# Local attention by chunk pairs with head pairs in the rows, instead of masked 128-token blocks

## The reference, cut to what matters

```python
qc = q.reshape(Bsz, n_chunks, CHUNK, B_KV_HEADS, groups, HEAD_DIM)
kb, vb = band(kc), band(vc)            # own chunk and the one before: 128 keys
scores = einsum('bcqhgd,bckhd->bchgqk', qc, kb) * (HEAD_DIM ** -0.5)
scores = where(valid, scores, -inf)    # the first chunk has none before it
m = maximum(max(scores, -1), sink)
p = exp(scores - m)
probs = p / (sum(p, -1) + exp(sink - m))
out = einsum('bchgqk,bckhd->bcqhgd', probs, vb)
```

## Time and profile before

| | |
|---|---|
| median of the runs | 906.06 us |
| the three runs | 903.81, 906.06, 906.17 us |
| span of the profiled execution, first to last instruction | 902.6 us |
| mean granted TensorE clock | 0.964 of full |
| busy: PE, PEld, DVE, ACT, POOL | 835.4, 678.3, 591.8, 410.8, 185.4 us |
| DMA | 144.43 MB, mean 160 GB/s |

### The profile page before, as it was taken

The page is one execution under the profiler, slowest core; times in us unless marked ns, Lnnn a source line. Parts: engine busy times, 40 slices in busy tenths (PEclk is TensorE's granted clock), DMA queues, the critical chain, the costliest instruction groups (busy, mean ns, idle before and its releaser), DMA issues.

```text
span 902.6 us, 11887 instructions
## 1 busy us (share of the span) xinstructions
PE 835.4 (93%) x3876; PEld 678.3 (75%) x3876; DVE 591.8 (66%) x827; ACT 410.8 (46%) x559; POOL 185.4 (21%) x116
## 2 busy tenths in 40 slices
PE   4997979699989999999979979887999899999998
PEld 3886757578868888888868867665788688888886
DVE  8799487976646646546378975788846565645643
ACT  4755245363535444444356634353543444443440
POOL 6244212624220000000024422423431200000000
PEclk8999889799999999999999979998999999999999
DMA  6743234354554656555654515252543556556641
GB/s 205 260 128 130 94 117 139 119 175 161 178 153 147 213 175 199 186 183 190 175 177 131 183 60 187 93 168 77 177 147 134 187 186 197 192 172 199 193 168 47
DMA packets 99091, 144.43 MB, mean 160 GB/s; under 512 B 11728, under 2 KB 62416, under 8 KB 99024
## 3 DMA queue, kind: packets, MB, share of 16 engines
q1 hardware_dynamic: 99024, 143.60, 49.2%
HBM read 142.54 MB, written 1.05 MB: 159 GB/s over the span
## 4 chain that ended last, share of the span: by engine, by line
PE 74%; DVE 10%; issue 8%; DMA 3%; ACT 3%; SPq 2%; DVEq 0%; ACTq 0%
PE big L1382 14%; PE big L1386 14%; PE big L1385 14%; PE mix L1382 9%; PE mix L1386 9%; PE mix L1385 9%; DVE w_lo L957 2%; DMA w_raw<-in_w_in 2%; DVE act_lo L974 1%; ACT w_hi L625 1%; SPq L538 1%; PE mix L1660 1%; DMA w_raw<-in_w_gate_up 1%; DVE row L1118 1%; DVE row L1121 1%
## 5 line engine op out<-in xcount | busy, mean ns | idle before, releaser
L625 ACT ACTIVATE w_hi<-w_raw 128x2048 fp32r<-128x2048 f32 (+2 forms) x140 | 256.2, 1835 | 168.4 <-DMA w_raw<-in_w_gate_up 108.3
L957 DVE TENSOR_TENSOR w_lo<-w_raw,w_hi 128x2048 fp32r<-128x2048 f32 (+2 forms) x108 | 242.9, 2264 | 42.5 <-ACT w_hi L625 42.0
L595 POOL TENSOR_TENSOR w_lo<-w_raw,w_hi 128x2048 fp32r<-128x2048 f32 (+2 forms) x36 | 147.1, 4096 | 441.8 <-ACT w_hi L625 441.8
L1382 PE MATMUL big<-w_hi,act_hi 128*128 128x512 f32 (+2 forms) x480 | 193.1, 402 | 18.8 <-DVE act_lo L974 10.0
L1385 PE MATMUL big<-w_lo,act_hi 128*128 128x512 f32 (+2 forms) x480 | 187.2, 390 | 0.0
L1386 PE MATMUL big<-w_hi,act_lo 128*128 128x512 f32 (+2 forms) x480 | 186.8, 389 | 0.0
L1382 PE MATMUL mix<-w_hi,act_hi 128*128 128x512 f32 x352 | 138.6, 394 | 7.6 <-DVE act_lo L974 7.6
L1386 PE MATMUL mix<-w_hi,act_lo 128*128 128x512 f32 x352 | 138.5, 394 | 0.0
L1385 PE MATMUL mix<-w_lo,act_hi 128*128 128x512 f32 x352 | 138.4, 393 | 0.0
L1382 PEld LDWEIGHTS big<-w_hi,act_hi 128*128 128x128 f32 x480 | 93.3, 194 | 44.0 <-issue 12.9
L1386 PEld LDWEIGHTS big<-w_hi,act_lo 128*128 128x128 f32 x480 | 92.8, 193 | 18.3
(11 more groups left out here) (189 smaller groups left out, 848.8 us busy)
## 6 DMA issues: line engine op xcount, KB each, us to landing
w_raw<-in_w_in SPq DMA_DIRECT2D x44, 1024.0 KB, 5.1
w_raw<-in_w_gate_up SPq DMA_DIRECT2D x88, 512.0 KB, 4.7
w_raw<-in_w_down SPq DMA_DIRECT2D x22, 1024.0 KB, 4.9
w_raw<-in_w_o SPq DMA_DIRECT2D x8, 1024.0 KB, 5.0
w_raw<-in_b_w_out SPq DMA_DIRECT2D x4, 1024.0 KB, 5.0
w_raw<-in_w_in SPq DMA_DIRECT2D x4, 904.0 KB, 6.3
w_raw<-in_w_in SPq DMA_DIRECT2D x4, 512.0 KB, 3.5
w_raw<-in_a_w_out SPq DMA_DIRECT2D x4, 512.0 KB, 4.0
```

The costliest lines, as they stand in the source:

```text
L595: nc.gpsimd.tensor_tensor(low(u)[:, a:b], arrived(u)[:, a:b], high(u)[:, a:b].bitcast(F32), ALU.subtract).then_inc(lo_by_pool.sem, 1)
L625: nc.scalar.activation(high(u), arrived(u), ACT.Copy).then_inc(hi_ready.sem, 1)
L957: nc.vector.tensor_tensor(low(u)[:, a:], arrived(u)[:, a:], high(u)[:, a:].bitcast(F32), ALU.subtract).then_inc(lo_by_dve.sem, 1)
L1382: ins = nc.tensor.matmul(dst[:, 0:w], xh, wh, start=first and n == 0, stop=False)
```

## The change

Only mixer B's attention changes. A row of 128 now is one chunk of 64 queries of two heads (a head pair), and meets just the chunk pair it may see: 128 keys, or 64 for the very first chunk. There is no mask and no logits copy: the maximum and the exponentials read the scores from PSUM. So a B unit has one block to transpose (turned_blocks), and Y goes to bank 3. The values of the middle chunk pair (chunks 1 and 2) stand in another tile, v_mid, which two DMAs fill from v_b. The sinks are laid out for the new rows by two DMAs instead of one. The S banks are now freed by the exponentials, not by the mask add. Cut to its core:

```diff
+def turned_blocks(i):
+    return 1 if ATTN[i][0] == "B" else ATTN[i][2] + 1
@@ mixer_uses
-        for k in range(tb + 1):
+        for k in range(turned_blocks(i)):
             uses.append((("T", i, k), 2 + k))
-        uses.append((("Y", i), 2))
+        uses.append((("Y", i), 3 if m == "B" else 2))
...
+        def chunk_keys(tb, cc):
+            return CHUNK if (tb, cc) == (0, 0) else 2 * CHUNK
@@ sync
-                    (sinks[:], b_sinks[l].partition_broadcast(P)),
+                    *((sinks[HD * a:HD * a + HD], b_sinks[l].rearrange(...)[a].partition_broadcast(HD))
+                      for a in range(2)),
+            def load_middle(l):
+                sp.wait_ge(*main_is_drained(l, "proj", "kv", 1))
+                sp.dma_start(v_mid[0:CHUNK], v_b[CHUNK:P, 0]).then_inc(mid_in.sem, 16)
+                sp.dma_start(v_mid[CHUNK:P], v_b[0:CHUNK, 1]).then_inc(mid_in.sem, 16)
...
+                    if u == FIRST["gate", "A", 0] + 2:
+                        load_middle(l)
@@ scalar, exps
+                    for odd in range(2):
+                        bank = mix_bank("S", i, odd)
+                        for cc in range(2):
+                            h, n = 2 * odd + cc, chunk_keys(tb, cc)
+                            e = nc.scalar.activation(probs[:, h, 0:n], mix[:, bank, cc * P:cc * P + n], ACT.Exp,
+                                                     scale=SCALE, bias=row[:, 1, h:h + 1], accum_out=row[:, 4, h:h + 1])
+                        e.then_inc(mix_drained[bank].sem, 1)
+                    return
@@ scalar, TQ: queries stored by chunk
-                    drain_pairs(l, "TQ", 3, 2)
+                    for kv in range(2):
+                        bank = mix_bank("TQ", kv)
+                        drain(l, chunked_queries(kv).rearrange("p (c a q) -> p a c q", a=2, q=CHUNK), "TQ", kv,
+                              src=mix[:, bank, :].rearrange("p (a c q) -> p a c q", a=2, q=CHUNK))
@@ vector, constants: the five memsets of mask_b are gone
@@ vector, softmax_in
+                if m == "B":
+                    first = mix_bank("S", i, 0)
+                    s_in = mix[:, first:first + 2, 0:2 * P].rearrange("p o (c k) -> p o c k", c=2)
...
+                    step(l, nc.vector.tensor_reduce(r0, s_in, AX_X, ALU.max))
...
@@ vector, softmax_out: the multiplication covers 64 and 128 keys (tb 0) or 4 x 128 (tb 1)
@@ tensor, Y of a B unit
+                            for cc in range(2):
+                                n, cols = chunk_keys(tb, cc), slice(kv * HD, (kv + 1) * HD)
+                                v = v_mid[:, cols] if (tb, cc) == (1, 0) else v_b[0:n, tb, cols]
+                                for odd in range(2):
+                                    dst = mix[HD * odd:HD * odd + HD, bank, 0:2 * P].rearrange("p (a t) -> p a t", a=2)
+                                    ins = nc.tensor.matmul(dst[:, :, cc * CHUNK:(cc + 1) * CHUNK], v,
+                                        probs_t[0:n, 0, 2 * odd + cc, :].rearrange("p (a t) -> p a t", a=2),
+                                        start=True, stop=True)
@@ tensor, S of a B unit: both banks free, then four matmuls of 128 queries by 128 keys
+                        for odd in range(2):
+                            pe.wait_ge(*mix_is_free(l, "S", i, odd))
+                        for cc in range(2):
+                            c = 2 * tb + cc
+                            for odd in range(2):
...
+                                ins = nc.tensor.matmul(dst, chunked_queries(kv)[half, c * P:(c + 1) * P], window,
+                                                       start=True, stop=True)
+                                if cc == 1:
+                                    ins.then_inc(mix_full[bank].sem, 1)
```

More of the change, by code:

```diff
@@ L153, in mixer_uses @@
              (("yaT",), 3), (("S", 0, 0), 0), (("S", 0, 1), 1), (("ydT", 0), 1), (("ydT", 1), 3)]
-    for i, (_, _, tb) in enumerate(ATTN):
+    for i, (m, _, tb) in enumerate(ATTN):
         if i + 1 < len(ATTN):
@@ L186 @@
 NORM_WIDTH = {n: {"K": 6, "Q": 8}.get(n[0], 2) for n in NORMS}
-N_PARAMS = 14
+N_PARAMS = 15
 POOL_IDENT = 2
@@ L194 @@
 TURNS = (0.0, 0.25)
-DVE_ANGLES = 8 + len(TURNS) + 2 + len(TWO_PI) + 2
+DVE_ANGLES = 3 + len(TURNS) + 2 + len(TWO_PI) + 2
 DVE_CONSTS = DVE_ANGLES + 2 + 2 * len(D_POOLS)
@@ L290, in trunk_kernel @@
         g_lat = sb("g_lat", [P, P])
-        sinks = sb("sinks", [P, 8])
+        sinks = sb("sinks", [P, 2, 2])
         b_sp = sb("b_sp", [P, A_GROUPS])
@@ L316, in trunk_kernel @@
         pos_in = sem("pos_in")
+        mid_in = signal("mid_in", 32)
         hi_ready = signal("hi_ready", NU)
@@ L431, in mask_cols, with chunked_queries @@
             return slice(0, P) if tb == 0 else slice(P, P + SEQ)
+        def chunked_queries(kv):
+            return qk_t[:, 3 + 2 * kv:5 + 2 * kv, :].rearrange("p a t -> p (a t)")
+        def chunk_keys(tb, cc):
+            return CHUNK if (tb, cc) == (0, 0) else 2 * CHUNK
         def score_view(bank, tb):
@@ L903, in _ @@
                                         ).then_inc(const_dve, 1)
-            done = 8 + len(TURNS)
+            done = 3 + len(TURNS)
             dve.wait_ge(const_dve, done)
@@ L1108, in softmax_in @@
                 m, kv, tb = ATTN[i]
-                mask = mask_b if m == "B" else mask_c
+                for odd in range(2):
+                    dve.wait_ge(*mix_is_full(l, "S", i, odd))
+                if m == "B":
+                    first = mix_bank("S", i, 0)
+                    s_in = mix[:, first:first + 2, 0:2 * P].rearrange("p o (c k) -> p o c k", c=2)
+                    r0, r1, r2 = (row[:, k, :].rearrange("p (o c) -> p o c", o=2) for k in range(3))
+                    sink = sinks[:, kv, :].unsqueeze(2).to_broadcast([P, 2, 2])
+                    step(l, nc.vector.tensor_reduce(r0, s_in, AX_X, ALU.max))
+                    step(l, nc.vector.scalar_tensor_tensor(out=r0, in0=r0, scalar=SCALE, in1=sink,
+                                                           op0=ALU.mult, op1=ALU.max))
+                    step(l, nc.vector.tensor_tensor(r2, sink, r0, ALU.subtract))
+                    nc.vector.tensor_scalar(row[:, 1, :], row[:, 0, :], -1.0, None, ALU.mult
+                                            ).then_inc(row_max.sem, 1)
+                    return
                 for odd in range(2):
                     bank = mix_bank("S", i, odd)
-                    dve.wait_ge(*mix_is_full(l, "S", i, odd))
                     nc.vector.tensor_tensor(logits[:, odd::2, 0:keys(tb)], score_view(bank, tb),
-                                            mask[:, mask_cols(tb)].unsqueeze(1).to_broadcast([P, 2, keys(tb)]),
+                                            mask_c[:, mask_cols(tb)].unsqueeze(1).to_broadcast([P, 2, keys(tb)]),
                                             ALU.add).then_inc(mix_drained[bank].sem, 1)
@@ L1118, in softmax_in @@
                 step(l, nc.vector.tensor_reduce(row[:, 0, :], logits[:, :, 0:keys(tb)], AX_X, ALU.max))
[L1119 to L1128, removed]
+                nc.vector.tensor_scalar(row[:, 1, :], row[:, 0, :], -SCALE, None, ALU.mult
+                                        ).then_inc(row_max.sem, 1)
@@ L1137, in softmax_out @@
                 step(l, nc.vector.reciprocal(row[:, 6, :], total))
-                p = probs[:, :, 0:keys(tb)]
-                nc.vector.tensor_tensor(p, p, row[:, 6, :].unsqueeze(2).to_broadcast([P, 4, keys(tb)]), ALU.mult
-                                        ).then_inc(probs_ready.sem, 1)
+                if m == "B" and tb == 0:
+                    parts = [(probs[:, cc::2, 0:chunk_keys(tb, cc)], row[:, 6, cc::2]) for cc in range(2)]
+                else:
+                    n = 2 * CHUNK if m == "B" else keys(tb)
+                    parts = [(probs[:, :, 0:n], row[:, 6, :])]
@@ L1142, in y_low @@
+                for p, r in parts:
+                    ins = nc.vector.tensor_tensor(p, p, r.unsqueeze(2).to_broadcast(list(p.shape)), ALU.mult)
+                ins.then_inc(probs_ready.sem, 1)
             def y_low(l, n, hi, lo, scale, *use, cols=N):
@@ L1454, in attention @@
                     if s == S_AT[i]:
-                        scores(l, ("S", i), tb, 3 + 2 * kv if m == "B" else 9, 7 + kv if m == "B" else 11)
+                        if m == "C":
+                            scores(l, ("S", i), tb, 9, 11)
+                            continue
+                        for odd in range(2):
+                            pe.wait_ge(*mix_is_free(l, "S", i, odd))
+                        for cc in range(2):
+                            c = 2 * tb + cc
+                            for odd in range(2):
+                                half = slice(HD * odd, HD * odd + HD)
+                                bank = mix_bank("S", i, odd)
+                                dst = mix[:, bank, cc * P:(cc + 1) * P].rearrange("p (d k) -> p d k", d=2)
```

(18 more changed lines are left out.)

35 lines of the change are left out of this document (19 added, 16 removed).

## The result

The changed kernel takes 889.45 us (median of 4 runs, 886.59 to 890.15), the kernel before on the same chip 904.93 (898.15 to 906.17): a ratio of 0.9846, 95% interval 0.9807 to 0.9884. The forecast was 888.0 in a range of 881 to 900. The profiled execution took 889.16 us with a span of 887.4, 15.2 under the span before; the mean granted clock was 0.965. In what follows the medians count every execution, and the ratios leave out those in a slower state (over 1.5% above the fastest of the same kernel).

A forecast was written before the change was run, and what follows sets the result against it. TensorE was taken as the bound, busy 835 of 902.6 us, with 26 us of waits for VectorE. Terms -5.5 - 4.2 - 3.0 - 5.0 - 0.8 + 0.5 = -18.0 us took 906.06 to 888, range 881 to 900.

The forecast's parts named there:

- the new wait at ydT: Slot 14: mixer D's matmul on TensorE waits for the last exponential, 2.0 us in the first layer, 1.5 in the second.
- the multiplication ahead of GpSimd: Slot 14: VectorE's multiplication of B's probabilities starts by 119.8, before GpSimd's subtraction at about 121.6, and takes 0.7 us.
- T(3): Slots 19 to 21, transposes of B unit 3's probabilities: earlier by 3.0 us in the first layer, 5.0 in the second.
- Slots 14 to 16, first layer: First unit's transposes and the chunk behind come earlier, net of the new wait: -5.5 us.
- Second layer: Same stage: the weight split isn't caught, its 3.2 us wait and 1.4 of slow clock go: -4.2 us.
- the price of the margin: Slots 19 to 21, second layer: if GpSimd catches VectorE again, the gain is -2 us in place of -5.0.
- Y(3) and behind: B unit 3's Y matmuls, columns halved: -0.4 us in each layer, -0.8 in the sum.
- SP's DMA at the start: First layer: one more small DMA on SP's queue ahead of unit 2's load costs +0.5 us.
- The rival of 894: Only the first stage gains, T(3) ending with GpSimd's last subtraction whatever comes before: -11.8 us; chance 0.2.
- The rival of 899: The wait at mixer D's matmul eats the savings, only part of the first stage's gain remaining: -7 us; chance 0.1.
- Slower: Slot 14: softmax_out(0) starts over 1.7 us later, GpSimd is first again: +4.4 us, 910; chance 0.06.

The follow-up runs named there:

- e3: Changed kernel with one more maximum (0.69 us of VectorE) in unit 3's softmax_in, ahead of D's merges; 891.8 us, 0.9856 of the kernel before.
- e10: Changed kernel unaltered, run again beside later variants on one chip; 890.3 us, 0.9875 of the kernel before.
- e2: Kernel before with only one added wait: mixer D's matmul waits for the first unit's exponentials; 897.01 us, 0.9931 of the kernel before.
- e8: Kernel before with the low parts of slots 17 and 22 computed by VectorE instead of GpSimd; 884.8 us, 0.9811 of the kernel before.
- e5: Changed kernel with slot 22's low parts computed by VectorE instead of GpSimd; 879.84 us, 0.9766 of the kernel before.
- after_again: Changed kernel unaltered, run once more; 888.42 us, 0.9816 of the kernel before.
- e1: Changed kernel with mixer D's matmul in banks 2 and 3, so it doesn't wait for the last exponential; 895.08 us, 0.9897 of the kernel before.
- e11: Changed kernel with slot 22's low parts on VectorE instead of GpSimd, more executions; 885.23 us, 0.9768 of the kernel before.
- e12: Changed kernel with slot 22's low parts on VectorE and mixer D's first matmul in bank 2, without its wait; 888.28 us, 0.9843 of the kernel before.

## Why the prediction was right

The mechanism came as forecast: the new wait at ydT, the multiplication ahead of GpSimd, and T(3) still waiting but earlier. That 889.45 lies only 1.4 us from the forecast is in part luck, since the kernel before took 904.93 this time and not 906.06: the gain is 15.5 us where 18 were forecast. One reading ahead of it is too narrow: beside the 26 us of the earlier trace rows, TensorE waits 17.6 us more for VectorE, at the low parts of the normed input (act_lo, L974), outside slots 14 to 21. No term rests on that.

Measured between the same instructions of both traces (S(0), T(1), T(3) and S(5) of each layer), forecast first:

- Slots 14 to 16, first layer: -5.5; S(0) to T(1) went from 35.38 to 29.62 us, -5.8. The new wait was forecast at 2.0 and is 2.23. The clock didn't fall behind it in either layer (I had taken half), and in e3 it did once.
- Second layer: -4.2; -4.3. The weight split is no longer caught, as forecast.
- T(3): -3.0 and -5.0; T(1) to T(3) went from 36.30 to 33.67 and from 38.41 to 33.70, -2.6 and -4.7. What I had wrong is the price of the margin: caught again, the first add was to cost 3 us (-2 in place of -5). e3 and e10 show 0.8 and 0.7, because the fourth add is then free: three subtractions catch three adds, whichever they are.
- Y(3) and behind: -0.8; -0.15 and -0.4.
- SP's DMA at the start: +0.5; S(0) is 1.15 us earlier. That isn't the change: the first matmul of the input projection starts at 15.63 in the kernel before, at 14.70 and 14.76 in e2 and e8, which have the same start, at 14.71 in the changed kernel, and at 15.44 in e5. From there to S(0) it is 88.57 us before and 88.34 after, so the extra issue cost TensorE nothing that can be seen.
- Not in the sum: from S(5) of the first layer to S(0) of the second the changed kernel loses 2.85 us, behind S(5) of the second 1.1 (269.25 us for 268.15; after_again has 269.34, e10 268.14, so this one comes and goes without any edit). These two and the start's -1.15 take the local -18.0 (forecast -18.5) to the span's -15.2.

The 2.85 are not chance alone. From C's last transpose to ydT of the second layer, less the wait there, the three kernels with the program before (before, e2, e8) take 348.7 to 349.2 us, and the eleven with the change's 350.0 to 355.8. The place is VectorE's first operations of the layer, before and after:

```profile
459.10 1.29 DVE L969 TENSOR_TENSOR sq<-mix,g_mix 128x512 f32<-128x512 f32 x2 [2.63 <-PE mix L1408]
```

```profile
450.63 0.69 DVE L995 TENSOR_TENSOR sq<-mix,g_mix 128x512 f32<-128x512 f32 x1 [2.47 <-PE mix L1447]
453.68 0.69 DVE L995 TENSOR_TENSOR sq<-mix,g_mix 128x512 f32<-128x512 f32 x1 [2.36 <-issue]
...
455.10 0.63 PE L1421 MATMUL big<-w_hi,act_hi 128*128 128x452 f32 x1 [3.86 <-DVE act_lo L1000]
```

Before (first fence) two operations follow each other; after, the second comes 2.36 us later though TensorE had finished what it reads (in the other traces with the change's program 1.3 to 4.1 us later, in e2 and e8 none), and TensorE waits 3.86 us for it and then runs at 1.2 GHz (matmuls 0.38 us apart for 452 columns). The profile gives no releaser; instruction transfers (its q14) fall in the same microseconds in both kernels. That VectorE's changed program is loaded later there is a guess that no run tested.

The rival of 894 had T(3) end with GpSimd's last subtraction. It does, 1.7 us before T(3) in the first layer (164.67), but before the change one merge, a longer multiplication and Y(2)'s low part stood behind that end (T(3) at 175.88 for 172.07) in the first layer. In the second a held operation of 3.76 us stood ahead of the merges, the gate chunk waited for them, and GpSimd's row of three subtractions had a pause of 4.51 us; after the change it runs through. Before and after:

```profile
607.76 9.51 POOL L595 TENSOR_TENSOR w_lo<-w_raw,w_hi 128x2048 fp32r<-128x2048 f32 x2 [4.51 <-ACT w_hi L625]
```

```profile
586.90 14.74 POOL L618 TENSOR_TENSOR w_lo<-w_raw,w_hi 128x2048 fp32r<-128x2048 f32 x3 [11.78 <-ACT w_hi L648]
```

Getting rid of these is the stage's gain. The rival of 899 is excluded by e1 and e2: the wait gives more than it costs. "Slower" is a real mechanism that e3 met once.

The Trainium skill (SBUF — State Buffer, section Who interferes with whom) has the engine that starts first keep the ports for its whole instruction: e5 and e11 agree, at 0.08 and 0.07 us either way. The Trainium skill (VectorE: DVE Perf Modes, section The TRN2 errata) gives VectorE 120 fixed cycles from PSUM against 58 from SBUF, an estimate of 65 ns more at its 0.96 GHz. They don't show: the maximum from PSUM took 689 ns, from SBUF 686.

## What to carry to other kernels

Where GpSimd and VectorE meet on SBUF operands, look at who starts first and by how much before pricing any saved work: here a wait of some 2 us gave 7.5, and one line that moved two subtractions gave about as much as a rewrite of the attention. Price a caught operation by the number of holding instructions in the row, not by how many operations get past. Where two starts lie within 0.1 us of each other, one trace and a median of four runs can mislead.

## What the runs showed of the hardware

- A GpSimd subtraction holds even a VectorE operation of 128x4 elements: 2.28 us at 107.31, and 4.54 in e11. It is held in its turn: 4.6 us alone, 5.31 when it starts 1.4 us behind VectorE's split of 2.28, and 6.69 when it starts 0.05 behind it (e12).
- One program on one chip gives times from 873.4 to 885.5 us (e11). Of 7.8 us between the traces of e5 and e11, 5.0 arise where GpSimd's start is 0.16 us earlier. Whether that one start makes the spread isn't shown.
- Eight traces have an idle gap at ydT in both layers, of 1.2 to 2.6 us. The granted clock stayed at 2.4 GHz at fourteen of the sixteen, one of 2.58 us (e2) among them. It fell to 1.2 at one of 2.13 us (e2, second layer) and one of 2.20 (e3, first). At T(3)'s 7.5 us it fell each of the five times.
